# Gather pipeline of a two-model transformer: nine gather slots, the top-16 lists in ten parts, and two query weight blocks kept between tiles

## What is computed

```python
mod = (cond @ w_ada[l] + b_ada[l])          # 6 x 1024 values
...
x = x + g1 * (y @ w_out[l])
h2 = rms_norm(x, norm2_g[l]) * (1.0 + sc2) + sh2
q = (h2 @ wq).reshape(T, 8, 2, 128)         # 8 heads, two halves
s = einsum('thpd,pnd->thpn', q, subkeys)    # 128 keys a half
top_s, top_i = top_k(s, 16)
cand = top_s[:, :, 0, :, None] + top_s[:, :, 1, None, :]
best_s, best_j = top_k(cand.reshape(T, 8, 256), 16)
expert, gate = i1 * 128 + i2, softmax(best_s)
a = gelu(h2 . u[expert]) * gate             # 128 experts a token
x = x + g2 * sum(a * v[expert])
```

## Time and profile before

| | |
|---|---|
| median of three runs | 2418.3 us (2417.24 to 2425.61) |
| profiled execution | 2418.6 us, its span 2416.8 us |
| PE busy | 2119.9 us, 88% |
| DVE busy | 1232.2 us, 51% |
| ACT busy | 823.8 us, 34% |
| POOL busy | 600.0 us, 25% |
| bytes moved by DMA | 772.25 MB, of which 570.46 MB through POOL's queue |
| granted clock of PE, mean | 0.951 |

### The profile page before, as it was taken

How to read it: one execution, slowest core, us unless ns; L and a number is a source line. 1 busy time by engine, 2 the same in 40 slices (tenths; PEclk the granted TensorE clock), 3 DMA queues, 4 the chain that set the end, 5 groups by cost and what they waited for, 6 DMA issues and landing times.

```text
span 2416.8 us, 24315 instructions
## 1 busy us (share of the span) xinstructions
PE 2119.9 (88%) x8264; PEld 1262.6 (52%) x8264; DVE 1232.2 (51%) x2915; ACT 823.8 (34%) x2356; POOL 600.0 (25%) x548
## 2 busy tenths in 40 slices
PE   7888999878989788889887789887999999989998
PEld 4554555434545344555433334435766666866665
DVE  2356777557677666587667576852630001441001
ACT  1234564334454434354444344541320001231000
POOL 1133343323343443233343435440000000000000
PEclk9889999999999988999998989998999999999999
DMA  9989999999999999999999999993343441253320
GB/s 394 408 329 410 410 427 414 427 426 414 426 427 409 410 427 378 381 417 427 412 427 390 418 423 422 427 425 141 139 175 124 172 157 63 85 207 126 153 117 18
DMA packets 108288, 772.25 MB, mean 320 GB/s; under 512 B 12274, under 2 KB 12546, under 8 KB 16003
## 3 DMA queue, kind: packets, MB, share of 16 engines
q0 software_dynamic: 78336, 570.46, 56.7%
q1 hardware_dynamic: 29828, 200.24, 20.9%
HBM read 769.61 MB, written 1.05 MB: 319 GB/s over the span
## 4 chain that ended last, share of the span: by engine, by line
PE 58%; DVE 20%; DMA 15%; ACT 3%; issue 2%; POOL 0%; DVEq 0%; SPq 0%; ACTq 0%; POOLq 0%
PE PS L511 57%; DMA BIG<-in_uv,EID 13%; DVE BIG L1581 7%; DVE BIG L1281 2%; DMA BIG<-in_wq 1%; DVE TI L1530 1%; DVE TI L1525 1%; DVE BIG L1277 1%; DVE BIG L1565 1%; DMA BIG<-in_win 1%; DVE TV L1528 1%; ACT DG L937 1%; PE PS L571 1%; DVE BIG L1526 1%; DVE TI L1546 1%
## 5 line engine op out<-in xcount | busy, mean ns | idle before, releaser
L511 PE MATMUL PS<-BIG,DG 128*128 128x512 f32 x2048 | 997.8, 630 | 195.9 <-ACT DG L937 163.9
L455 POOL DMA_INDIRECT BIG<-in_uv,EID x512 | 582.8, 1138 | 908.4 <-PE PS L511 866.1
L1581 DVE CUSTOM_DVE_ANT_0 BIG<-BIG,H 128x1024 f32<-128x1024 f32 x512 | 627.7, 1226 | 347.6 <-DMA BIG<-in_uv,EID 302.2
L511 PEld LDWEIGHTS PS<-BIG,DG 128*128 128x128 f32 x2048 | 386.4, 199 | 691.6 <-issue 366.5
L511 PE MATMUL PS<-HT,BIG 128*128 128x128 f32 (+1 forms) x2304 | 386.3, 325 | 16.5 <-DMA BIG<-in_wq 12.2
L511 PEld LDWEIGHTS PS<-HT,BIG 128*128 128x128 f32 x2304 | 352.8, 194 | 84.8 <-issue 46.9
L511 PE MATMUL PS<-BIG,HT 128*128 128x256 f32 (+3 forms) x1216 | 306.0, 411 | 20.2 <-DMA BIG<-in_win 9.6
L1126 ACT ACTIVATE AV<-AV 128x1 f32<-128x1 f32 x512 | 102.6, 200 | 554.0 <-DVE AV L1581 553.2
L511 PEld LDWEIGHTS PS<-BIG,HT 128*128 128x128 f32 x1216 | 236.2, 200 | 92.4 <-issue 50.8
L511 PE MATMUL PS<-BIG 128*128 128x512 f32 (+7 forms) x792 | 277.5, 518 | 3.9 <-ACT BIG L1012 2.1
L1281 DVE TENSOR_TENSOR BIG<-BIG 128x256 f32<-128x256 f32 (+1 forms) x96 | 49.3, 514 | 383.5 <-ACT BIG L1262 381.3
(11 more groups left out here) (161 smaller groups left out, 1182.8 us busy)
## 6 DMA issues: line engine op xcount, KB each, us to landing
BIG<-in_win SPq DMA_DIRECT2D x36, 1024.0 KB, 4.9
BIG<-in_wada POOLq DMA_DIRECT2D x32, 1024.0 KB
BIG<-in_wq SPq DMA_DIRECT2D x32, 1024.0 KB
BIG<-in_wup SPq DMA_DIRECT2D x32, 1024.0 KB, 6.9
BIG<-in_wdn SPq DMA_DIRECT2D x32, 1024.0 KB, 4.8
BIG<-in_wout SPq DMA_DIRECT2D x24, 1024.0 KB, 5.6
BIG<-in_wada SPq DMA_DIRECT2D x16, 1024.0 KB
BIG<-in_uv,EID POOLq DMA_INDIRECT x512
```

What stands on the lines that cost most here:

```text
L455: pool.e.indirect_dma_start(out=slot(u), out_offset=None, in_=I[f"uv{l}"], in_offset=bass.IndirectOffsetOnAxis(ap=EID[:, t * 128 + j:t * 1 ...
L511: return pe.e.matmul(dst, a, b, start=start, stop=stop)
L1581: v.e.tensor_tensor_reduce(out=JD, in0=slot(u)[:, 0:1024], in1=H[:, t, :], scale=1.0, scalar=0.0, op0=ALU.mult, op1=ALU.add, accum_out=AV[ ...
```

## The change

The parts, in the order of the diff:

- A ninth gather slot in columns 0 to 2,047 of `MOD`. The condition columns, biases and the replicated condition `CREP` that lay there move to the front of `PARB`, whose parameter loads now bring columns 1,024 to 3,719 only. The second model's projections are laid out anew behind it, with the latents in `LAT`.
- The late blocks of layer 1 begin at iteration 106 instead of 97. The next tile's mixer begins at iteration 2 (4 in tile 1) instead of 4 (18 in tile 0). Heads 0 and 1 of the next tile start at 92 and 106, heads 2 to 7 at 1, 17, ..., 81. The output weights follow each other by two steps instead of three.
- `finish` stands before the third dot of the new tile instead of behind it.
- The second tile of a layer takes head 7-h where it took head h. Its first two heads then use the weights of heads 7 and 6, which lie in place from the first tile: they aren't loaded again, and their two slots are held until the second tile has read them.
- DVE's part of a head is cut at steps 10 to 19 (ten parts), the gate's last step at 21 instead of 16. At the start `early` keeps its ten steps 8 to 17, while the heads' steps go on to 22.
- In the second model `project` of B0 and B1 is cut in halves of the tokens. Both first halves come before the transposes of tile 1, into banks of their own (`FIRST`). D0 comes behind the window slabs at r=4, D1 at r=6. The first scores wait for the copies of B0 and B1; SP waits for the last modulation block before it loads the second model's parameters.

```diff
-GSLOTS = list(range(8))
+GSLOTS = list(range(8)) + [12]
...
-LATE = [97 + 2 * i for i in range(12)] + [2 * 129 + 10 + 2 * i for i in range(4)]
+LATE = [106 + 2 * i for i in range(12)] + [2 * 129 + 10 + 2 * i for i in range(4)]
...
-        CREP = MOD[:, 128:384].rearrange("p (k m) -> p k m", k=8)
+        CREP = PARB[:, 128:384].rearrange("p (k m) -> p k m", k=8)
...
-            return RNG[:, u * SLOT:(u + 1) * SLOT]
+            return RNG[:, u * SLOT:(u + 1) * SLOT] if u < SLOTS else MOD[:, 0:SLOT]
...
-                    sp.e.dma_start(PARB, I["par1"][1].partition_broadcast(128)).then_inc(*landed("ld_par", 1))
+                    sp.e.dma_start(PARB[:, 1024:PAR], I["par1"][1, 1024:PAR].partition_broadcast(128)).then_inc(*landed("ld_par", 1))
...
-                load(in_w, ("wq", l, t, h), I["wq"][l * 8 + h], 2048, ("pe.q", l, t, h))
+                if t == 0 or h > 1:
+                    load(in_w, ("wq", l, t, h), I["wq"][l * 8 + (h if t == 0 else 7 - h)], 2048,
+                         ("pe.q", l, t, h) if t > 0 or h < 6 else ("pe.q", l, 1, 7 - h))
...
                 sp.wait_ge(*at("v.h2", 1, 1))
+                sp.wait_ge(*at("a.ada", 1, 23))
...
                 if k >= 10:
                     next(h1, None)
-                if k >= 8:
+                if 8 <= k < 18:
                     next(early)
...
                 for b in range(129):
-                    experts(p, b)
                     if p > 0 and b == 2:
                         finish(p - 1)
-                    if b % 16 == 3 and b < 96:
+                    experts(p, b)
+                    if b % 16 == 1 and b < 96:
...
-                        if b == (18 if p == 0 else 4):
+                        if b == (4 if p == 1 else 2):
                             live.append(pre(*TILES[p + 1]))
-                        if b in (102, 115):
-                            live.append(head(*TILES[p + 1], 0 if b == 102 else 1))
+                        if b in (92, 106):
+                            live.append(head(*TILES[p + 1], 0 if b == 92 else 1))
...
-                wv = have(in_w, ("wq", l, t, h)).rearrange("p (k n) -> p k n", k=8)
+                wv = have(in_w, ("wq", l, t, h) if t == 0 or h > 1 else ("wq", l, 0, 7 - h)).rearrange("p (k n) -> p k n", k=8)
...
+            def project(l, name, parts=(0, 1)):
+                for t in parts if name in FIRST else range(2):
                     have_hT(2 + l, t, 0)
...
             for l in range(L):
                 if l > 0:
                     project_A(l, 0)
+                project(l, "B0", (0,))
+                project(l, "B1", (0,))
                 transposes(2 + l, 1, 0, ("v.n1", l, 1))
                 project_A(l, 1)
-                project(l, "B0")
-                project(l, "B1")
+                project(l, "B0", (1,))
+                project(l, "B1", (1,))
...
-                    elif r == 3:
-                        project(l, "D0")
                     elif r == 4:
                         slabs_T("wT", l, 0, 3)
                         slabs_T("wT", l, 1, 3)
-                    elif r == 5:
+                        project(l, "D0")
+                    elif r == 6:
                         project(l, "D1")
...
                     v.e.match_replace(js, w[:, 0:8], s, TINY).then_inc(*up("v.c"))
+                    yield from k.to(WHEN["top"] + 1 + 2 * p)
                     own()
...
-                    yield from k.to(WHEN["top"] + 1 + p)
+                    yield from k.to(WHEN["top"] + 2 + 2 * p)
...
                 v.e.max(w[:, 0:8], cd).then_inc(*up("v.c"))
+                yield from k.to(WHEN["top"] + 5)
...
+                yield from k.to(WHEN["top"] + 6)
                 v.wait_ge(*at("v.best", l, t, h))
                 v.e.max_index(ix[:, 8:16], w[:, 8:16], js).then_inc(*up("v.c"))
-                yield from k.to(WHEN["top"] + 3)
...
                 for z in range(2):
+                    yield from k.to(WHEN["top"] + 7 + z)
+                    own()
...
+                yield from k.to(WHEN["top"] + 9)
                 own()
                 sel = JS[:, 320:352]
```

More of the change, by code:

```diff
@@ L36 @@
 EARLY = 32
-LATE = [97 + 2 * i for i in range(12)] + [2 * 129 + 10 + 2 * i for i in range(4)]
+LATE = [106 + 2 * i for i in range(12)] + [2 * 129 + 10 + 2 * i for i in range(4)]
 BATCH = {(1, 8): (0, 1), (1, 20): (1, 0)}
 PROJ = (2, 3, 4, 0, 1)
-WHEN = dict(T0=3, proj=7, qk=17, qkT=22, pool=26, s0=30, pw=32, s1=34, pT0=36, pT1=40, pv0=41, pv1=45, T1=54, out=58,
-            n2=71, T2=74, end=78, sk=6, top=10, head=17, enter=88)
+LAST = [GSLOTS[(EARLY + 512 + i) % len(GSLOTS)] for i in range(len(GSLOTS))]
+WHEN = dict(T0=3, proj=7, qk=17, qkT=22, pool=26, s0=30, pw=32, s1=34, pT0=36, pT1=40, pv0=41, pv1=45, T1=53, out=57,
+            n2=71, T2=74, end=78, sk=6, top=10, head=22, enter=88)
 class Clock:
@@ L161 @@
 SECTIONS = ("b", "a", "c", "d")
+FIRST = dict(B0=2, B1=3)
 CHUNK = dict(a=0, b=1, c=2, d=3)
@@ L185, in build @@
         DG = sb("DG", 4 * 128)[:, :].rearrange("p (b n) -> p b n", b=4)
-        CREP = MOD[:, 128:384].rearrange("p (k m) -> p k m", k=8)
-        MC, BC, NC = MOD[:, 0:32], MOD[:, 32:64], MOD[:, 64:80]
+        CREP = PARB[:, 128:384].rearrange("p (k m) -> p k m", k=8)
+        MC, BC, NC = PARB[:, 0:32], PARB[:, 32:64], PARB[:, 64:80]
         SC = sb("SC", 384)[:, :]
@@ L235, in build @@
         JD2 = PRJ[:, 2048:2304]
-        prj2 = MOD[:, 0:3776].rearrange("p (t n) -> p t n", t=2)
-        RT = MOD[:, 3776:4800]
-        TMP = MOD[:, 4800:5120]
+        RT, TMP = MOD[:, 0:1024], MOD[:, 1024:1344]
+        prj2 = MOD[:, 1344:4416].rearrange("p (t n) -> p t n", t=2)
+        LAT = MOD[:, 4416:5120].rearrange("p (t n) -> p t n", t=2)
         RB = G2.rearrange("p (t n) -> p t n", t=2)
@@ L345, in pre @@
                     if (l, t) == (0, 0) and i == 2:
-                        sp.e.dma_start(PARB, I["par1"][0].partition_broadcast(128)).then_inc(*landed("ld_par", 0))
+                        sp.e.dma_start(PARB[:, 1024:PAR], I["par1"][0, 1024:PAR].partition_broadcast(128)).then_inc(*landed("ld_par", 0))
                 yield from k.to(WHEN["pool"])
@@ L353, in pre @@
                 for j in range(4):
-                    yield from k.to(WHEN["out"] + 3 * j)
+                    yield from k.to(WHEN["out"] + 2 * j)
                     load(in_w, ("wout", l, t, j), I["wout1"][l * 4 + j], 2048, ("pe.out", l, t, j))
@@ L366, in sp_program @@
             sp.e.dma_start(CST, I["cst"]).then_inc(*landed("ld_cst"))
-            sp.e.dma_start(MOD[:, 32:80], I["cols"]).then_inc(*landed("ld_cols"))
+            sp.e.dma_start(PARB[:, 32:80], I["cols"]).then_inc(*landed("ld_cols"))
             sp.wait_ge(*at("v.zero"))
@@ L378, in enter @@
                 in_2.held.update(in_w.held)
-                for i in range(len(GSLOTS)):
-                    in_2.held[GSLOTS[(EARLY + 512 + i) % len(GSLOTS)]] = ("pe.vsum", 3, 128 - len(GSLOTS) + i)
+                for i, u in enumerate(LAST):
+                    in_2.held[u] = ("pe.vsum", 3, 128 - len(LAST) + i)
                 load_A(0)
@@ L757, in pe_program @@
             drive(pre, head, early(), late(), experts, lambda p: None, enter)
-            def project(l, name):
-                for t in range(2):
+            def project(l, name, parts=(0, 1)):
+                for t in parts if name in FIRST else range(2):
                     have_hT(2 + l, t, 0)
                 w = have(in_2, ("w2", l, name)).rearrange("p (k n) -> p k n", k=8)
[L764 to L767, removed]
+                if name in FIRST:
+                    bk = singles.where[("prj", l, name)] = FIRST[name] if l == 0 else FIRST[name] - 2
+                    if l > 0:
+                        pe.wait_ge(*at("v.xf", l - 1, 0))
+                else:
+                    bk, freed = singles.take(("prj", l, name), (EVAC[name] + ".prj", l, name))
+                    if freed:
+                        pe.wait_ge(*at(*freed))
+                for z in parts:
                     zs = slice(z * 128, (z + 1) * 128)
@@ L773, in project @@
                             p = mm(PS[:, bk, z * 256:(z + 1) * 256], HT[:, k, zs], w[:, k, :], k == 0, k == 7)
-                p.then_inc(*up("pe.prj", l, name))
+                if 1 in parts:
+                    p.then_inc(*up("pe.prj", l, name))
             def latent_T(l, t):
@@ L1497, in pre @@
                 for j in range(4):
-                    yield from k.to(WHEN["out"] + 3 * j + 3)
+                    yield from k.to(WHEN["out"] + 2 * j + 3)
                     v.wait_ge(*at("pe.out", l, t, j))
```

36 lines of the change are left out of this document (17 added, 19 removed).

## The result

| | before | after |
|---|---|---|
| median of the runs made beside each other, us | 2418.8 | 2392.5 (2389.1 to 2395.9) |
| ratio, 95% interval | | 0.9888 (0.9867 to 0.9908) |
| span of the profiled execution, us | 2416.8 | 2394.1 |
| end of the last expert product, us | 1646.9 | 1622.5 |
| from there to the end, us | 769.9 | 771.6 |

The change makes the kernel 1.1% faster; forecast were 2,393 us and 1.0%. The two last lines already say that the sum came out right by errors that cancel, which is luck. The forecast had 17.4 us from the gather stretch and 8 from the second model. The trace has 24.4 and -1.7.

The account below looks back on a forecast made before the run. DMA bytes were taken to bound the kernel up to 1,644 us, a chain through PE after it. Terms 9.8 + 1.2 + 1 + 7.9 + 2.5 - 5 + 7 + 1 = 25.4 us gave 2,393 us, range 2,381 to 2,408.

Parts of the forecast that it names:

- Query weights: Gather stretch: four query weight loads of 1,024 KB go away, 2.46 us each at 427 GB/s, 9.8 us won.
- Parameter loads: Two parameter loads each lose 512 KB: 1.2 us won in the saturated stretch, 1 us before 143 us.
- Boundaries: Second and third tile boundary: PE's wait shrinks and DMA no longer idles, 7.9 us won, bounds 4 and 12.7.
- Ninth slot elsewhere: Between 970 and 990 us, where PE waits for a projection weight: one more slot wins 2.5 us, bounds 0 and 4.4.
- Long lists between dots: Gather stretch: cutting DVE's 6.4 us head block into parts of at most some 1.5 us is worth nothing.
- Start: Head 0's first index list comes 7.6 us later under ten parts: 5 us lost, bounds 3 and 8.
- Kept slots: Two of four weight slots held until the next tile's heads read them: zero cost, 6 us as bound.
- Layer 0's entry: Second model: halves of B0 and B1 fill PE's 7.27 us wait for tile 1's norm, 7 us won.
- D0 and D1: Second model's rounds, both blocks one place later: net gain 0.5 us per layer, 1 in all, bounds -3 and +4.
- the weight ring: Rival: with two slots held, late blocks at iterations 110 to 128 load late and DMA idles: 2,406 us, chance 0.10.
- DMA isn't the bound: Rival: PE bounds the gather stretch, so bytes and idle DMA are worth nothing: 2,415 us, chance 0.06.
- The late lists: Rival: index lists come too late and POOL starves; at 2 us idle DMA per list 2,441 us, chance 0.04.

Follow-up runs that it names:

- experiment 3: The changed kernel with all 32 query weight blocks loaded, none kept for the second tile: median 2404.4 us.
- experiment 6: The changed kernel with lists in the old four parts, next tile's heads 0 and 1 at iterations 102 and 115, all query weights loaded: median 2410.2 us.
- experiment 4: The changed kernel with eight gather slots instead of nine: median 2397.8 us.
- experiment 5: The changed kernel with all 32 lists in the old four parts, heads still beginning at the changed kernel's iterations: median 2392.7 us.
- experiment 10: The changed kernel with lists in four parts and eight gather slots, heads at the changed kernel's iterations: median 2400.3 us.
- experiment 2: The changed kernel with head (0,0,0) alone in the old four parts, so its index list is written early: median 2384.9 us.
- experiment 7: The changed kernel with B0 and B1 of the second model whole again, behind tile 1's transposes: median 2405.5 us.
- experiment 9: No new edit: traces of twelve kernels compared from layer 0's to layer 1's feed-forward part; less half the half-rate time, 377.7 to 378.5 us remain.
- the five: The five kernels sharing the changed gather code, the changed kernel among them: last expert product ends at 1619.2 to 1626.4 us, mean 1622.3.

## Why the prediction was right, and where it was not

- **Query weights, 9.8:** 9.6 by A (experiment 3). Right. The trace agrees with bytes at 427 GB/s; the Trainium skill's 358 GB/s ("DMA: Bandwidth & Descriptors", Bandwidth) would make it 11.7, and slices at 427 exclude it as a limit here. The same section gives that figure as a core's share while both cores of a memory domain stream, and 425 GB/s for one that streams alone, as this one does.
- **Parameter loads, 2.2:** not tried by itself.
- **Boundaries, 7.9:** 6.6 by A, 9.4 by the two windows (experiment 6). Right. The share had hidden part of it, as the forecast's upper bound allowed. The cause is the earlier begin of heads 0 and 1.
- **Ninth slot elsewhere, 2.5 (0 to 4.4):** 5.7 by A and 4.2 by the windows (experiment 4), more than forecast; over its bound by A, though by less than one A is known. The place was wrong as well. It was to cover the knot, and covers it not at all; it fills small dips all over the stretch.
- **Long lists between dots, 0:** right for the steady stretch and wrong for the first 40 us. Long lists with an early start cost 6.1 us by A, most of it in one dip (experiment 5). With eight slots they bring small dips back in the steady stretch too (experiment 10). The window that I took for proof, 510 to 550, is one without a dip.
- **Start, -5:** -4.8 by A, -7.6 by medians (experiment 2). Right.
- **Kept slots, 0:** right; experiment 3 shows no gain from giving them up. In 480 to 560 us PE does wait 4.9 us for modulation weights, while the slice stands at 427 GB/s.
- **Layer 0's entry, 7 (2.7 to 8.4):** 9.2 in B (experiment 7), a little over its upper bound. By the forecast's own terms the lower bound is 3.2 and not 2.7; nothing hangs on it. The halves ran at full clock from their first product; I had let the clock rise only after 4 us.
- **Layer 1's entry, 0:** right.
- **D0 and D1, +1 (-3 to +4): the step that failed.** I had the waits right (1 to 2 us in round 3; measured 1.47), and left out what a wait does to the clock behind it. In the profiled execution C is 9.7 us longer than with the blocks back, and by the sum of experiment 9 all of it is time at half rate; B and C together are 2 to 13 us longer over all kernels, and the median 6.7. The rule for it stood in my own text, used for layer 0's entry only.

The common error behind the slot term is the measure. The DMA share of 10 us windows before, from 160 to 1,610 us, lacks 16.9 us; GB/s against 427 lacks 41.0. After, it is 8.0 and 17.9. Eighteen of the windows of before moved only 354 to 398 GB/s at a share of 0.93 to 1.00, and look full or nearly so by share. Between the two profiled executions A won 24.4 us (forecast 17.4), B 9.7 (7 and half a microsecond) and C lost 11.4 (won half a microsecond): 22.7 in all, against 25.4 forecast and 26.3 between the medians.

The terms by A close to a few us: 9.6 (reload) + 2.2 (parameter loads, as forecast) + 6.6 (burst) + 13.9 (cuts4_8) - 4.8 (start) = 27.5 against 24.6 for the mean of the five. Of the rivals, the weight ring and "DMA isn't the bound" fell by experiment 3. The late lists fell by the profile: POOL waits for EID once, at the start.

What stays open is why the same wait costs the clock in one execution and layer and not in another. No edit here kept the waits and changed only what precedes them. That three kernels share one pattern (B 149.7, C 391.4; in b_whole B is longer by its own edit) and three others have another (154.5 and 383.5) may mean that it isn't chance alone; one trace of each can't tell.

## What to carry over

Cost a stretch that is bound by transfers by the bytes that it falls short of its best rate, not by the DMA share, and look for the one place where a buffer is still empty, such as the start: a finer cut is worth most there, and so is an early begin. When a filler is moved away from a PE wait in a chain that PE sets, price the wait and then the matmuls behind it at half rate as well. A right total proves nothing until the stages are right one by one.

## What the hardware showed that I had not expected

- A wait of 1.47 us in a PE that had been busy 19.9 of the 20 us before was followed by 1.2 GHz; so was one of 2.08 us. A granted clock of 0.74 and of 0.66 over 20 us, mixed from full and half rate, makes 10 and 14 us at half rate. The Trainium skill ("TensorE: Matmul & The Clock Gate", Part 1) says that an idle PE falls to half rate; the trace agrees, but the same wait left it at full rate elsewhere.
- The length of the wait doesn't say what it costs. Windows of the changed kernel, 20 us each behind a wait of 1.48 us (layer 0), 2.25 us (entry of layer 1), 1.47 us and 2.08 us (layer 1):
```profile
1681.90:1701.90 20.00, 20.00 (x115) 17.66 (x116) 11.91 (x26) 8.34 (x29) 0.00 (x0) 1.00 0.46 171
1998.40:2018.40 20.00, 19.08 (x103) 18.03 (x104) 3.11 (x10) 2.25 (x10) 0.00 (x0) 0.91 0.10 42
2063.80:2083.80 20.00, 19.97 (x90) 17.24 (x90) 11.63 (x24) 6.57 (x22) 0.00 (x0) 0.76 0.24 83
2100.00:2120.00 20.00, 19.99 (x88) 17.34 (x88) 10.28 (x22) 9.18 (x28) 0.00 (x0) 0.66 0.01 4
```
- An execution with the same waits can lose its clock in layer 0 (B 154.5 instead of 149.5 us) or in layer 1 (C 391.4 instead of 383.5).
